# Retention step of a two-layer decoder trunk: the sample queries' products with the past states, with stationary and moving side swapped

## What is computed

```
att = einsum('nhid,nhjd->nhij', qc_, kc_) * d_in
o = einsum('nhij,nhjv->nhiv', att, vc_) + einsum('nhid,nhdv->nhiv', qc_ * q_dec[..., None], s)
```

## Time and profile before

| | us |
|---|---|
| median of 3 runs | 1453.36 |
| lowest, highest | 1450.92, 1453.76 |
| profiled execution, its own time | 1445.9 |
| its span | 1443.9 |

### The profile page before, as it was taken

One profiled execution on the slowest core, in us unless ns is written; L12 is line 12 of the kernel. 1 busy time (PEld: TensorE's weight loads), 2 busy tenths in 40 slices (PEclk: granted clock), 3 DMA queues, 4 the chain that ended last, 5 costly groups with the idle time before them and its releaser, 6 DMA issues.

```text
span 1443.9 us, 28417 instructions
## 1 busy us (share of the span) xinstructions
PE 1360.1 (94%) x11165; PEld 1306.2 (90%) x11165; DVE 812.1 (56%) x870; ACT 650.0 (45%) x715; POOL 216.7 (15%) x343
## 2 busy tenths in 40 slices
PE   6999999899877999999999999989997789999998
PEld 4999999899656899999999999989984579999998
DVE  4655545477673665554455555456867546555454
ACT  4655533334223565553355554432434245555433
POOL 3000001370334100000100000034313611000001
PEclk9999999999988999999999999999999899999998
DMA  6444445753758344444444444475637744444443
GB/s 207 150 145 145 143 160 180 209 166 115 219 179 277 118 145 146 151 152 144 152 142 156 152 145 135 158 236 142 208 110 221 258 153 146 145 145 145 142 153 121
DMA packets 210895, 235.27 MB, mean 163 GB/s; under 512 B 14974, under 2 KB 203144, under 8 KB 210804
## 3 DMA queue, kind: packets, MB, share of 16 engines
q1 hardware_dynamic: 200828, 204.90, 43.8%
q0 software_dynamic: 9856, 29.14, 6.4%
q10 hardware_dynamic: 120, 0.03, 0.0%
HBM read 228.83 MB, written 5.32 MB: 162 GB/s over the span
## 4 chain that ended last, share of the span: by engine, by line
PE 84%; issue 7%; DVE 5%; DVEq 1%; POOLq 1%; DMA 1%; ACT 1%; POOL 0%; SPq 0%; ACTq 0%
PE ps L1235 21%; PE ps L1237 21%; PE ps L1236 21%; PE ps L1317 4%; PE ps L1319 4%; PE ps L1318 4%; PE ps L1457 2%; DVE kbuf L990 1%; PE ps L1495 1%; PE ps L1402 1%; DVEq L1165 1%; PE ps L1630 1%; DVE h_lo L851 0%; DVE w_lo L844 0%; DMA x_tok<-in_x_sample 0%
## 5 line engine op out<-in xcount | busy, mean ns | idle before, releaser
L587 ACT ACTIVATE w_hi<-w_raw 128x2048 fp32r<-128x2048 f32 x170 | 325.6, 1915 | 554.6 <-PE ps L1237 427.3
L844 DVE TENSOR_TENSOR w_lo<-w_raw,w_hi 128x2048 fp32r<-128x2048 f32 x170 | 391.4, 2303 | 210.4 <-ACT w_hi L587 207.7
L1235 PE MATMUL ps<-h_hi,w_hi 128*128 128x320 f32 x768 | 241.0, 314 | 9.5 <-DVE w_lo L844 3.5
L1236 PE MATMUL ps<-h_lo,w_hi 128*128 128x320 f32 x768 | 239.7, 312 | 0.0
L1237 PE MATMUL ps<-h_hi,w_lo 128*128 128x320 f32 x768 | 239.5, 312 | 0.0
L1235 PE MATMUL ps<-g_hi,w_hi 128*128 128x320 f32 x704 | 218.4, 310 | 1.2 <-DVE g_lo L851 1.2
L1237 PE MATMUL ps<-g_hi,w_lo 128*128 128x320 f32 x704 | 217.7, 309 | 0.0
L1236 PE MATMUL ps<-g_lo,w_hi 128*128 128x320 f32 x704 | 217.7, 309 | 0.0
L1236 PE MATMUL ps<-act_lo,w_hi 128*128 128x320 f32 x704 | 217.5, 309 | 0.0
L1235 PE MATMUL ps<-act_hi,w_hi 128*128 128x320 f32 x704 | 217.5, 309 | 0.0
L1237 PE MATMUL ps<-act_hi,w_lo 128*128 128x320 f32 x704 | 217.5, 309 | 0.0
(11 more groups left out here) (275 smaller groups left out, 1923.4 us busy)
## 6 DMA issues: line engine op xcount, KB each, us to landing
w_raw<-in_ffn_w_in SPq DMA_DIRECT2D x90, 1024.0 KB, 5.1
w_raw<-in_ffn_w_out SPq DMA_DIRECT2D x32, 896.0 KB, 4.6
kbuf<-in_cache_k SPq DMA_DIRECT2D x128, 192.0 KB, 3.3
w_raw<-in_w_in SPq DMA_DIRECT2D x22, 1024.0 KB, 5.7
w_raw<-in_ffn_w_out SPq DMA_DIRECT2D x16, 1024.0 KB, 5.0
kbuf<-in_cache_v POOLq DMA_DIRECT2D x64, 192.0 KB, 4.4
w_raw<-in_w_out SPq DMA_DIRECT2D x8, 1024.0 KB, 7.5
v_c<-in_cache_v POOLq DMA_DIRECT2D x32, 192.0 KB, 3.4
```

What stands on the lines that cost most here:

```text
L587: act.activation(w_hi[:, slot, :], w_raw[:, slot, :], ACT.Copy).then_inc(hi_done, 1)
L844: dve.tensor_tensor(w_lo[:, slot, :], w_raw[:, slot, :], w_hi[:, slot, :].bitcast(F32), ALU.subtract).then_inc(split_done, 1)
L1235: pe.matmul(out, w_hi[:, slot, w], hi[:, k, :], start=(k == 0), stop=False)
L1236: pe.matmul(out, w_hi[:, slot, w], lo[:, k, :], start=False, stop=False)
```

## The change

`q_dec` is filled with head a in column group a. `past_states()` makes four products for a head pair instead of nine: the stationary side is now 32 columns of `q_dec` (two sequences by two heads by 8 tokens), the moving side 128 columns of the state (the same two sequences by 64 channels), and the outputs go to the 32 partitions of strip g. The result is token-major: a row for each sequence, head and token, and for each of the two sequences a block of 64 columns, of which a row needs one. VectorE copies even and odd blocks to two tiles, `o_past0` and `o_past1`. `ret_out` puts the samples' own product first and then, for each head, multiplies both tiles as the stationary side by 32 columns of the identity in four strided runs of 8, which picks the rows wanted and writes them channel-major to strided runs of 8 columns of bank 6.

```diff
--- before.py
+++ after.py
@@ -180,7 +180,7 @@
         pt_s = [at("pt_s0", [P, 9 * 96], F32, arena_at, 54), tmp[:, 0:864]]
         o_tok = at("o_tok", [96, 2, P], F32, arena_at, 57.5)
         att_s = [at(f"att_s{n}", [SMP, SMP], F32, arena_at, kb) for n, kb in enumerate((58.5, 58.75, 71, 71.25))]
-        o_past = at("o_past", [P, 3, SMP], F32, arena_at, 59)
+        o_past = [at("o_past0", [P, 3, HD], F32, zone_at, 13.5), at("o_past1", [P, 3, HD], F32, arena_at, 59)]
         q_dec = at("q_dec", [P, 3, NB, 2, NT], F32, arena_at, 59.75)
         s0 = at("s0", [P, 3, NB, HD], F32, arena_at, 61.25)
         o_sq = at("o_sq", [P, 3, TOK], F32, arena_at, 67.25)
@@ -1086,7 +1086,7 @@
                 for a in range(2):
                     o = HD * a
                     for f in range(3):
-                        ins = dve.tensor_tensor(q_dec[o:o + HD, f, :, 1 - a, :],
+                        ins = dve.tensor_tensor(q_dec[o:o + HD, f, :, a, :],
                                                 z[o:o + HD, ZQR + f, SEQ:].rearrange("p (b t) -> p b t", b=NB),
                                                 cst["q_decay"][o:o + HD, f, :].rearrange("p (b t) -> p b t", b=NB), ALU.mult)
                 ins.then_inc(q_dec_ok, 1)
@@ -1108,10 +1108,8 @@
                 turn_k(1, 1, 1)
                 evac_last(9)
                 dve.wait_ge(past_done, L + 1)
-                for a in range(2):
-                    o = HD * a
-                    ins = dve.tensor_copy(o_past[o:o + HD, :, :].rearrange("p f (b t) -> p f b t", b=NB),
-                                          ps[o:o + HD, 3, 0:384].rearrange("p (f b a t) -> p f b a t", f=3, b=NB, a=2)[:, :, :, 1 - a, :])
+                for half in range(2):
+                    ins = dve.tensor_copy(o_past[half][:], ps[:, 3, 0:384].rearrange("p (f b v) -> p f b v", f=3, b=2)[:, :, half, :])
                 ins.then_inc(past_ok, 1)
                 mix_lo(11)
                 normalise(4)
@@ -1396,12 +1394,9 @@
                     wait_apart(pe, q_dec_ok, L + 1)
                     for f in range(3):
                         q = q_dec[:, f, :, :, :].rearrange("p b a t -> p (b a t)")
-                        pe.matmul(ps[HD:P, 3, P * f:P * f + NT], s0[:, f, 0, :], q[:, 0:NT], start=True, stop=True)
-                        for b in range(NB - 1):
-                            c = 2 * NT * b + NT
-                            pe.matmul(ps[:, 3, P * f + c:P * f + c + 2 * NT], s0[:, f, b:b + 2, :].rearrange("p b v -> p (b v)"),
-                                      q[:, c:c + 2 * NT], start=True, stop=True)
-                        ins = pe.matmul(ps[0:HD, 3, P * f + P - NT:P * f + P], s0[:, f, NB - 1, :], q[:, P - NT:P], start=True, stop=True)
+                        for g in range(4):
+                            ins = pe.matmul(ps[32 * g:32 * g + 32, 3, P * f:P * f + P], q[:, 32 * g:32 * g + 32],
+                                            s0[:, f, 2 * g:2 * g + 2, :].rearrange("p b v -> p (b v)"), start=True, stop=True)
                     ins.then_inc(past_done, 1)
 
                 def ret_scores(h):
@@ -1431,9 +1426,13 @@
                     for s, r, c in heads:
                         pe.matmul(ps[r, 6, 128:256], vr_tok[:, 1, c], att_p[s % 4][:, 256:384], start=False, stop=True)
                     for s, r, c in heads:
-                        pe.matmul(ps[r, 6, 256:320], ident[:, r], o_past[:, f, :], start=True, stop=False)
+                        pe.matmul(ps[r, 6, 256:320], vr_tok[0:SMP, 2, c], att_s[s % 4][:], start=True, stop=False)
                     for s, r, c in heads:
-                        ins = pe.matmul(ps[r, 6, 256:320], vr_tok[0:SMP, 2, c], att_s[s % 4][:], start=False, stop=True)
+                        for b in range(2):
+                            at_q = 16 * b + 8 * (s % 2)
+                            ins = pe.matmul(ps[r, 6, 256:320].rearrange("p (g b t) -> p g b t", g=4, b=2)[:, :, b, :], o_past[b][:, f, :],
+                                            ident[:].rearrange("p (g x) -> p g x", g=4)[:, :, at_q:at_q + 8],
+                                            start=False, stop=(b == 1))
                     ins.then_inc(or_done, 1)
 
                 def smp_state(f):
```

## The result

| | before | after |
|---|---|---|
| median, us | 1450.39 (6 runs) | 1439.78 (6 runs) |
| lowest, highest, us | 1448.64, 1453.76 | 1439.13, 1442.09 |
| profiled execution, us | 1445.9 | 1442.09 |
| its span, us | 1443.9 | 1440.1 |

The ratio is 0.9925 with a 95% interval of 0.991 to 0.9939: 9 to 13 us faster, 10.6 by the medians. I had forecast 4.6 us and a range that ended at 1444.5. The sign was right, the size was not. One thing in the table is odd and leads to the cause: the two profiled executions are only 3.8 us apart.

A forecast was written before the change was run, and what follows sets the result against it. TensorE was taken to bound the kernel, with 84% of the chain, and VectorE to be late next. -8.5 + 1.2 + 2.7 = -4.6 us, from a median of 1453.36 to 1448.8 us; range 1444.5 to 1452.8.

The forecast's parts named there:

- Part 1: past_states(): 24 records in 1.0 us (0.7 to 2.8), TensorE saving 5.1 us a layer; clock stays up through mix(9).
- Part 2: Copies to o_past start 5.2 us earlier in layer 0, 3.3 in layer 1, limited by VectorE: -8.5 us together.
- Part 3: VectorE's two copies to o_past, same elements for each partition, old pair 0.71 us: no change in time.
- Part 4: ret_out(): eight records of 32 columns for four of 64, 0.2 us a call, six calls: +1.2 us.
- Part 5: Scores behind the longer wait before sample_scores(1) (3.8 and 4.2 us): clock falls, 1.35 us a layer, +2.7 us.
- theory B: Posed after the measurement, no chance given: the changed kernel gains in a place that the traces don't show.
- Clock stays up behind the wait: Rival, chance 0.18: no clock fall at the scores behind the wait before sample_scores(1); -7.3 us, 1446.1 us.
- A long fall behind it: Rival, chance 0.15: clock stays down 6.1 us behind that wait, slowing mix(10) too; -1.6 us in all, 1451.8 us.
- Strided pieces slow: Rival, chance 0.05: in ret_out() every strided record runs alone, 12 us more; kernel slower by 6.2 us, 1459.6 us.
- Savings lost: Rival, chance 0.07: past_states() or VectorE's chain yields only half of the 8.5 us or less; -0.4 us with the clock's price.

The follow-up runs named there:

- e4: Kernel before, with 21 of its 27 past-state products given 128 moving columns instead of 16 (past term wrong): 1443.58 us, ratio to before 0.9957.
- e10: Changed kernel with the twelve products of past_states() done four times over, same results: 1437.86 us, ratio to before 0.9927.
- e6: Changed kernel with ret_out()'s strided pieces ahead of the samples' own product, both heads' even pieces before the odd ones: 1438.29 us, ratio 0.9917.
- e3: Changed kernel with five extra float32 products of 384 columns in the wait before sample_scores(1), results thrown away: 1437.79 us, ratio 0.9916.
- e5: Changed kernel run and profiled again without an edit: 1440.01 us median of 12, ratio to before 0.9936.
- e7: Changed kernel with ret_out()'s pieces unstrided, one run of 32 columns read and written (past term wrong): 1440.17 us, one run.

## Why the prediction was wrong in its size

**Part 1, past_states().** Right. 24 records in 0.86 us where I took 1.0, the clock full through mix(9). e4 adds the reason of the old fall, which I had read from what TensorE did before it. It began in past_states() itself in all eight passes, and past_states() then took up to 8.9 us for the 6.1 that I took.

**Part 2, what reaches the end.** The mechanism was right: VectorE is late next, the cover is 2.9 us by the changed kernel's rows (e10 used 2.0 of it), and all that follows moves along. The size failed: this is the step that puts the forecast off most. I wrote 5.2 + 3.3 = 8.5 us; the mean is 11.3. The 3.3 of layer 1 came from one draw of a fall that lasts 3.4 us in some executions and 10.2 in others, and the very same profile had 6.8 us in layer 0. Two layers run the same code, so the difference of 5.2 and 3.3 was the sign that the number is drawn, and I added them as if they were measurements of two places. VectorE's chain sets the new start whatever the clock does, so the changed kernel gives nothing of a long fall back: the longer the old one, the more is won. Of the 2.8 us that were missing (11.3 - 8.5) the draw of before is 1.6 us (11.3 - 9.7), and 0.3 is the changed kernel's own first profile (24.84 us for both layers, mean 24.56). The remaining 0.9 can be followed. 0.5 is VectorE's chain, which I read 0.23 us too long for each layer (4.36 for 4.13). 0.25 lies behind the copies' start: the scores came 1.3 us after it and now come 1.16 after it. 0.2 lies ahead: the key turn starts 0.05 and 0.18 us earlier after the start of past_states().

**Part 3, the copies.** Near: 0.61 us for 0.71. They are on the chain, so the tenth counts in each layer (it is in the 0.25 us above).

**Part 4, ret_out().** Too low: 2.1 us for 1.2 by calls at the full clock, 2.6 with the third calls as they are. With a change of shape taken off, a record of half the columns costs 0.033 us, not the 0.05 that I kept; with the order of e6, where the two halves of the array take turns, 0.026. e6 also changes what stands ahead of these records, so that the turns make this difference is a reading and not shown. What I left out are the two further changes of tile shape at 0.10 us each (in the changed kernel a group of four records lasts 394.58 - 394.32 = 0.26 us in front of a change of shape; in e6, where the same four records come last and are followed by their like, 393.49 - 393.33 = 0.16). I had weighed that rule of the Trainium skill (TensorEngine Tiling, Key Properties) and set it aside, since the change of shape in before seemed to cost nothing. The runs agree with the page, which gives no time for it: with the 0.1 us that I had estimated the sum would have said 2.4. The row that misled me held four records of 64 columns in 0.21 us, which by e6's pace need 0.11 and one change of 0.10.

**Part 5, the clock behind the wait.** The mechanism was right (e3), the wait 3.6 and 3.8 us for 3.8 and 4.2. The size was near for a fall (1.4 to 1.5 us), but before paid something there as well. At the full clock its score group took 4.6 to 5.5 us to the next product, where e10's took 4.2, with idle time inside the group (0.60 us in the row at 363.62) for which the profile names no releaser. Taken together, from the scores' start to ret_scores(0), before took 18.43 us (mean of eight), the changed kernel 19.29 (mean of four), 0.86 us a layer and not 1.35. So 1.7 for 2.7 us.

**The sum.** -11.3 + 2.1 + 1.7 = -7.5 us by the traces, -7.0 with the third calls. The mean spans of the profiles say the same: 1446.5 us over four of before, 1438.7 over two of after, -7.8. The timed medians say -10.6 and -9.2; the interval of the second holds -7.5, that of the first (-8.9 to -13.1) does not. Over all 76 timed runs of before and 18 of the changed kernel the means are 1448.9 and 1440.0 us, 9.0 apart with a standard error of 0.8. So 1 to 2 us between the traces and the timed runs stay open, and that is all the place that is left for theory B; both kernels have ten or more other lower-clock stretches in each execution, and six profiles are too few to average them.

**The reference point and the range.** Of the 9.0 us between 1448.8 and the measured 1439.78, 3.0 are the reference: 1453.36 was the median of three runs, and six gave 1450.39. The other 6.0 are the saving. I took the median as 7.5 us above the profiled execution and let every term stand. But an execution that far below the others is itself the warning: its terms for the very thing that varies are low ones. The range had to hold a term of up to 19.6 - 12.3 = 7.3 us a layer; it gave a microsecond for all clock falls. The bounds that it names add up to 1446.1 - 1.2 - 1.0 = 1443.9, a little below the 1444.5 that I wrote, and neither reaches 1439.78.

**The rivals.** Clock stays up behind the wait: no, though e3 shows what it is worth. A long fall behind it: in one layer of four (e5), and it ended at 358.3, ahead of mix(10), so it did not cost what the rival had put on mix(10). Strided pieces slow: refuted by e7, and with it the first sentence of the Trainium skill's Advanced Engine Details and Errata, PSUM Cachelines, for runs of 8; its second sentence, that two neighbours suffice, agrees. Savings lost: no, both layers gave theirs in full.

## What to carry to other kernels

Where a profile holds the same code twice (layers, iterations) and a stretch takes 16 us in one and 18 in the other, the difference may be a spread, as it was here: take more profiles of the kernel before, or put the spread into the range. Loads of 128 stationary columns for 16 moving ones cost twice in this kernel, once in their own time and once in the clock of the dense work behind them; swapping the sides and using strips mended both. When an engine's work gets shorter, look at once at the order of the engine that it now waits for: moving two copies up gave 7.8 us, where the change gave some 9.

## What the runs showed of the hardware that was not expected

- The same kernel on the same chip spread over 14 us (1442.06 to 1456.2), and the mean granted clock of the runs (0.975 and 0.963 at these ends) and the profiles tie it to the lower-clock stretches: 16.34 to 19.64 us for one and the same piece of code.
- TensorE was busy throughout and the clock still fell: behind loads of 128 columns with 16 moving ones in all eight passes of before (0.51 over 3.50 us with 3.50 busy), and with 128 moving ones in neither layer of e4.
- Superfluous products that shortened the wait, 36 ahead of it in e10 and 5 within it in e3, left the clock of the scores at its full level at no loss of time; with 3.57 us idle ahead of them it was 0.50.
- A change of tile shape costs about 0.10 us of TensorE: the four records of line 1427 take 0.32 us ahead of one (394.32 - 394.00) and 0.21 ahead of none (e6, 393.02 - 392.81). Strided runs of 8 float32 columns cost nothing (e7).
- Records of 64 outputs and 32 columns went at 0.026 us in e6, where the two column halves alternate, and at 0.033 in the changed kernel, where the same half comes twice in a row. That the halves are the reason is not shown.
